# Moving three recurrence units under an earlier projection, with the weights split by column blocks and the rows kept tile by tile

## The reference, cut to what matters

```
h    = layer_norm(x)
q, k, v, x_lru, y_lru = split(h @ w_in)          # widths 512, 128, 128, 512, 512
q, k = rope(rms_norm(q)), rope(rms_norm(k))      # per head of 64
xc   = 4-tap depthwise conv of x_lru along the sequence
r, i = sigmoid(xc @ wa + ba), sigmoid(xc @ wx + bx)       # per head, two directions
a    = exp(-8 r softplus(-lambda));  u = sqrt(1 - a^2) * i * xc
h_fwd, h_bwd = first-order recurrences h = a h + u, forwards and backwards
lru  = (h_fwd + h_bwd) * gelu(y_lru)
```

## Time and profile before

| What | Value |
|---|---|
| profiled execution, its own time | 1866.18 us |
| its span on the core | 1864.5 us |
| granted TensorE clock, mean | 0.91 |
| TensorE busy | 1527.2 us (82%) |
| VectorE busy | 1164.1 us (62%) |
| ScalarE busy | 890.2 us (48%) |
| POOL busy | 512.8 us (28%) |
| stage A, hi part of a tile (L361), 16 times | 1.02 us each |
| stage A, lo part of a tile (L327), 16 times | 1.22 us each |
| stage A, addition on POOL (L294), 16 times, median | 2.39 us each |
| stage A, eviction (L376), 64 times | 0.38 us each |

### The profile page before, as it was taken

The page is one execution under the profiler, slowest core; times in us unless marked ns, Lnnn a source line. Parts: engine busy times, 40 slices in busy tenths (PEclk is TensorE's granted clock), DMA queues, the critical chain, the costliest instruction groups (busy, mean ns, idle before and its releaser), DMA issues. The chain is left out here.

```text
span 1864.5 us, 29928 instructions
## 1 busy us (share of the span) xinstructions
PE 1527.2 (82%) x8888; PEld 1300.7 (70%) x8889; DVE 1164.1 (62%) x2119; ACT 890.2 (48%) x1440; POOL 512.8 (28%) x352
## 2 busy tenths in 40 slices
PE   3999976878854999999999999982599999999700
PEld 3999964656544888888888888861477778778500
DVE  7644339889866866766666677635754444544177
ACT  3323224765674655555555555521255544655222
POOL 2112104342340011121111112111454443545236
PEclk9999988989977999999999999985699999999855
DMA  6655544443414121111112111105378777885562
GB/s 237 225 200 203 195 114 130 142 136 116 144 56 155 45 75 52 51 51 73 52 52 79 51 51 51 63 34 180 113 229 265 218 190 220 236 242 110 101 267 115
DMA packets 143232, 247.96 MB, mean 133 GB/s; under 512 B 18240, under 2 KB 100160, under 8 KB 141120
## 3 DMA queue, kind: packets, MB, share of 16 engines
q1 hardware_dynamic: 115280, 159.59, 25.5%
q0 software_dynamic: 12528, 45.62, 10.4%
q10 hardware_dynamic: 15360, 41.95, 5.8%
HBM read 152.75 MB, written 94.37 MB: 133 GB/s over the span
## 5 line engine op out<-in xcount | busy, mean ns | idle before, releaser
L1312 DVE TENSOR_TENSOR d_probs_t_lo<-d_pt_ps,d_probs_t_hi 128x512 fp32r<-128x512 f32 x256 | 164.2, 683 | 118.7 <-ACT d_probs_t_hi L1254 118.0
L1254 ACT ACTIVATE d_probs_t_hi<-d_pt_ps 128x512 fp32r<-128x512 f32 x256 | 139.3, 596 | 151.6 <-PE d_pt_ps L1141 145.3
L107 PE MATMUL acc<-k_hi,wl_hi 128*128 128x256 f32 x512 | 148.7, 290 | 20.0 <-DVE k_lo L327 9.6
L1298 DVE TENSOR_REDUCE d_neg_max<-d_s_ps 128x1 f32<-128x1024 f32 x128 | 155.3, 1213 | 5.7 <-PE d_s_ps L1130 5.7
L1159 PE MATMUL d_ot_ps<-d_probs_t_hi,d_v_split 128*128 128x256 f32 x512 | 139.2, 306 | 13.1 <-DVE d_probs_t_lo L1312 10.7
L107 PE MATMUL e_a_ps<-up_hi,e_xt_hi 128*128 x336 | 138.9, 413 | 12.9 <-issue 10.6
L108 PE MATMUL acc<-k_lo,wl_hi 128*128 128x256 f32 x512 | 147.3, 288 | 0.0
L109 PE MATMUL acc<-k_hi,wl_lo 128*128 128x256 f32 x512 | 147.2, 288 | 0.0
L1237 ACT ACTIVATE d_probs<-d_s_ps,d_neg_max 128x1024 f32<-128x1024 f32 x128 | 143.2, 1119 | 3.6 <-DVE d_neg_max L1298 3.6
L1141 PE MATMUL d_pt_ps<-ident,d_probs 128*128 128x128 f32 x1024 | 134.2, 274 | 4.4 <-ACT d_probs L1237 3.2
L108 PE MATMUL e_a_ps<-up_lo,e_xt_hi 128*128 x336 | 134.7, 401 | 0.0
(11 more groups left out here) (300 smaller groups left out, 4176.6 us busy)
## 6 DMA issues: line engine op xcount, KB each, us to landing
up_raw<-in_exp_w SPq DMA_DIRECT2D x32, 1024.0 KB, 10.3
down_raw<-in_exp_w SPq DMA_DIRECT2D x16, 1024.0 KB, 11.7
h_dram<-d_h_tile SPq DMA_DIRECT2D x17, 512.0 KB, 2.7
sum_dram<-d_h_tile SPq DMA_DIRECT2D x17, 512.0 KB, 3.5
h_dram<-v_all ACTq DMA_DIRECT2D x16, 512.0 KB, 3.8
ht_hi_dram<-k_hi ACTq DMA_DIRECT2D x8, 1024.0 KB, 5.3
ht_lo_dram<-k_lo ACTq DMA_DIRECT2D x8, 1024.0 KB, 6.6
c_hi<-ht_hi_dram SPq DMA_DIRECT2D x16, 512.0 KB
```

The source lines that it names most:

```text
L107: pe.matmul(out, lhs[0], rhs[0], start=first, stop=False)
L1254: act.activation(pt_hi[:, c * HALF:(c + 1) * HALF, h % 2], pt_ps[c][:], ACT.Copy).then_inc(pth_done[c], 1)
L1298: dve.tensor_reduce(nm[:, u, h:h + 1], s_ps[h % 2][:], AX, ALU.max, negate=True).then_inc(nm_done, 1)
L1312: dve.tensor_tensor(pt_lo[:, part, h % 2], pt_ps[c][:], pt_hi[:, part, h % 2].bitcast(F32), ALU.subtract)\
```

## The change

Stage A becomes `project_xy`. The functions of a unit move into a class `Lru`, which both stages use. The first three units run in stage A beside chunks 4 to 7 (the first sequence is complete after chunk 3), the other five in stage B, one for three tiles (`EVERY = 3`). In stage A:

- The weights are loaded and split in four blocks of 256 columns (all 8 row blocks at once), in place of eight row blocks; products of feature blocks 0 and 1 need only the first.
- Four accumulators become two; the two banks that come free are the gates' `gp`. One `xy` buffer in place of two. The unit's large tiles lie in the raw weights' space.
- The two tiles of a chunk share one chain of small VectorE instructions (`stats` and the rest are twice as wide).
- The transposes of the next chunk follow feature block 3 (block 5 in chunk 0). The loops are written out.
- The small vectors, gate weights and softplus move here, between tile loads 5 and 6 and behind chunks 2 and 3.
- `ht_hi_dram` and `ht_lo_dram` hold one tile per entry, so that stage B reads a tile in whole rows.

In stage B a step is one tile: the rsqrt chain runs for each tile, and the orders of all queues are new. The parts of a unit are spread over three steps.

The core of the diff (the class `Lru` holds the unit's old instructions unchanged; what is only moved is left out):

```
-        acc = [ps(f"acc{j}", [P, 512]) for j in range(4)]
+        acc = [ps(f"acc{j}", [P, 512]) for j in range(2)]
+        gp = [ps(f"gpa{j}", [P, 512]) for j in range(2)]
...
+            transpose(0)                                  # TensorE, stage A
+            for c in range(NC):
+                for f in range(NF):
+                    project(c, f)                         # waits acc_free >= 8c + f - 1
+                    if f == turned_after(c) and c + 1 < NC:
+                        transpose(c + 1)
+                j = c - FIRST                             # FIRST = 4
+                if 0 <= j < len(units):
+                    if j == 0:
+                        pe.wait_ge(gw_in, 128)
+                    lru.gates(pe, j, units[j])
...
+            split(0)                                      # ScalarE, stage A
+            normalise(0)
+            split(1)
+            store_lo = turn(0)
+            split(2)
+            split(3)
+            store_lo()
+            normalise(1)
+            for c in range(NC):
+                j = c - FIRST
+                if 0 <= j - 1 < len(units):
+                    lru.root(act, j - 1)
+                for f in range(NF):
+                    evict(c, f)
+                    if f == turned_after(c):
+                        if c + 1 < NC:
+                            store_lo = turn(c + 1)
+                        if c + 2 < NC:
+                            normalise(c + 2)
...
+                if 0 <= j < len(units):
+                    lru.tanhs(act, j, units[j])
+                    lru.decays(act, j, units[j])
...
+            norms(0); split(0); gain(0); turn(0)          # VectorE, stage A (one per line)
+            split(1); norms(1); split(2); gain(1); split(3)
+            for c in range(NC):
+                j = c - FIRST
+                if j == 0:
+                    lru.conv(dve, link, 0, units[0])
+                if j >= 0 and j + 1 < len(units):
+                    lru.conv(dve, link, j + 1, units[j + 1])
+                if 0 <= j - 1 < len(units):
+                    lru.factor(dve, j - 1)
+                if c + 1 < NC:
+                    turn(c + 1)
+                if 0 <= j - 1 < len(units):
+                    lru.scans(dve, link, j - 1)
+                    lru.output(dve, j - 1)
+                if c + 2 < NC:
+                    norms(c + 2)
+                    gain(c + 2)
...
+                if 0 <= j < len(units):
+                    lru.gated_x(dve, j)
...
-            for g in range(PERIODS):                      # TensorE, stage B
-                front(2 * g)
-                if g:
-                    back(2 * g - 2)
-                front(2 * g + 1)
-                if g:
-                    back(2 * g - 1)
-                gates(g)
+            for t in range(NT):
+                front(t)
+                if t:
+                    back(t - 1)
+                if t % EVERY == 1 and t // EVERY < len(units):
+                    lru.gates(pe, t // EVERY, units[t // EVERY])
...
+            for t in range(NT):                           # ScalarE, stage B
+                if t:
+                    split(t - 1)
+                if t % EVERY == 0 and 0 < t // EVERY <= len(units):
+                    lru.root(act, t // EVERY - 1)
+                square(t)
+                if t:
+                    evict(t - 1)
+                if t % EVERY == 1 and t // EVERY < len(units):
+                    lru.tanhs(act, t // EVERY, units[t // EVERY])
+                    lru.decays(act, t // EVERY, units[t // EVERY])
...
+            for t in range(NT):                           # VectorE, stage B
+                j = t // EVERY
+                if t:
+                    rotate(t - 1)
+                if t % EVERY == 0 and 0 < j <= len(units):
+                    lru.scans(dve, link, j - 1)
+                if t % EVERY == 1:
+                    if 0 < j <= len(units):
+                        lru.output(dve, j - 1)
+                    if j + 1 < len(units):
+                        lru.conv(dve, link, j + 1, units[j + 1])
+                if t % EVERY == 2 and j < len(units):
+                    lru.gated_x(dve, j)
+                    lru.factor(dve, j)
+                norms(t)
```

More of the change, by code:

```diff
@@ L304, in ln, with norms @@
+            def norms(c):
                 for j in range(2):
@@ new lines, in norms, with gain @@
+                link(last)
+                if c:
+                    dve.wait_ge(xn_done, 2 * c)
+                link(dve.tensor_scalar(var[:], mv[:, :, 1], LN_EPS, None, ALU.add))
+                rsqrt(dve, link, var[:], rstd[:], tmp[:])
+                link(dve.tensor_tensor(tmp[:], mv[:, :, 0], rstd[:], ALU.mult))
+                dve.tensor_scalar(shift[:], tmp[:], -1.0, None, ALU.mult).then_inc(stats_done, 1)
+            def gain(c):
+                for j in range(2):
+                    t = 2 * c + j
+                    dve.wait_ge(xn_done, t + 1)
+                    if c:
+                        dve.wait_ge(h_stored[j], 16 * c)
+                        dve.wait_ge(tr_done, t - 1)
+                    else:
+                        dve.wait_ge(ln_sem, 32)
@@ new lines, in _ @@
+            norms(0)
+            split(0)
+            gain(0)
+            turn(0)
+            split(1)
+            norms(1)
+            split(2)
+            gain(1)
+            split(3)
+            for c in range(NC):
+                j = c - FIRST
+                if j == 0:
+                    lru.conv(dve, link, 0, units[0])
[3 more added lines that the diff above has]
+                    lru.factor(dve, j - 1)
+                if c + 1 < NC:
+                    turn(c + 1)
[5 more added lines that the diff above has]
+                    gain(c + 2)
+                if c == 2:
+                    abs_lam()
+                if c == 3:
+                    softplus()
+                if 0 <= j < len(units):
+                    lru.gated_x(dve, j)
@@ L757, in _ @@
-            root(NU - 1)
-            evict(NT - 2)
+            for t in range(NT):
+                if t:
[8 more added lines that the diff above has]
+                    lru.decays(act, t // EVERY, units[t // EVERY])
@@ L759, in _ @@
+            split(NT - 1)
             evict(NT - 1)
@@ L859, in rotate @@
                 dve.tensor_tensor(rt[u], rt[u], rb[u], ALU.add).then_inc(rt_done, 1)
[L861 to L876 removed]
+            lru.conv(dve, link, 0, units[0])
+            for t in range(NT):
+                j = t // EVERY
+                if t:
[11 more added lines that the diff above has]
+                norms(t)
+            rotate(NT - 1)
+            if NT // EVERY == len(units) and NT % EVERY == 1:
+                lru.output(dve, len(units) - 1)
         @block.gpsimd
         def _(pool):
[L880 removed]
             pool.wait_ge(rows_in, 48)
@@ L916, in split @@
                                    k_st[u][:, 0].bitcast(F32), ALU.subtract).then_inc(lo_done, 1)
-            for g in range(PERIODS):
-                for step in (swap, split):
-                    for t in (2 * g, 2 * g + 1):
-                        step(t)
+            for t in range(NT):
+                swap(t)
+                split(t)
 def need(eng, sem, value):
```

735 lines of the change are left out of this document (350 added, 385 removed).

## The result

The changed kernel takes 1943.04 us (median of four runs, 1940.96 to 1948.18), the kernel before 1864.0 beside it: a ratio of 1.0432, 95% interval 1.04 to 1.0464. The forecast was 1941. The profiled execution took 1943.3 us, with a span of 1941.6 and a mean granted clock of 0.893 (0.91 before).

The account below looks back on a forecast made before the run. TensorE bounds the first projection and VectorE the second stage, with a ring through ScalarE close behind. Stage A +93.7 and stage B -16.4, together +77.3, on the median 1863.38 gave 1941 us; 8-in-10 range 1893 to 1970.

Parts of the forecast that it names:

- Start: Start of stage A: TensorE's first product at 25.4 us instead of 32.68, 7.3 us sooner, a lead that doesn't last.
- second gain: VectorE's second gain instruction before the first product: 3.46 us, because POOL's addition stands beside it.
- Ordinary chunks: Stage A, chunks 1 to 4: block 6 waits 6.8 us for evict 4, clock loses 1.7, making 33.3 us a chunk.
- slow starts: TensorE after each stall in stage A: lower granted clock loses 1.7 us a stall.
- rival (4): TensorE's clock stays low after each stall through two blocks, 4.1 us more at ten stalls: 1982 us, chance 0.08.
- rival (3): First chunks of stage A don't stall, two accumulators being enough, 5 x 8.5 us less: 1898 us, chance 0.08.
- Chunks with units: Stage A, chunks 5 to 7: copies wait behind unit work and norms; 60.6, 41.3 and 39.5 us, last product at 340.6.
- Table loads: ScalarE's table loads: 1.28 us each; the skill page's extra drain, an estimated 23 us in all, left out.
- Stage B: Second stage: 52.7 us per three tiles, 302.1 us in all, a change of -16 us.
- my two terms: Stage B on VectorE: eight more chains, 22 us, and a 4.2 us root wait in each period.
- Rival (1): Both stages: units fill idle time and nothing waits, stage A +1, stage B -59 us: 1805 us, chance 0.09.
- Rival (2): Stage B's ring is looser than worked out and waits vanish, 43 us less: 1898 us, chance 0.10.

Follow-up runs that it names:

- norms ahead: Changed kernel with norms and normalise of chunk c + 2 ahead of the transposes of chunk c + 1 on VectorE and ScalarE: 1891.9 us.
- four banks: Changed kernel with four accumulators instead of two for chunks 0 to 3, queue order unchanged: 1918.4 us.
- root first: Changed kernel with the root in stage B ahead of the split on ScalarE: 1931.7 us.
- pairs in B: Changed kernel with stage B back in periods of two tiles, its five units in the first five periods: 1917.2 us.
- best A with pairs in B: Changed kernel with norms ahead, stage A's decays and root later on ScalarE, and stage B in periods of two tiles: 1850.1 us.

## Why the prediction was right, step by step

- **Start.** First product 25.4 forecast, 24.31 measured. The second gain took 1.22 us (at 14.18), not 3.46: POOL's first addition, which I had put ahead of it, began 0.24 us behind it (at 14.42), and it was POOL's that stretched. Chunk 1 started at 60.94 (64.3), block 2 at 34.86 (36.8). A small miss, never made up: the products of chunk 4 ended at 196.1 (199.2), 3.1 us early.
- **Ordinary chunks.** From the start of chunk 1 to the end of chunk 4 it took 135.2 us (134.9 forecast), 33.8 a chunk. The gaps were 6.01, 5.26, 6.69 and 7.21, mean 6.3 (6.8 forecast; its terms add up to 14.2 and not 14.3, so 6.7). The stretch holds five slow starts, one behind the gap ahead of chunk 1, as in the forecast, and 10.8 us are left for them (135.2 less four times 24.8 and the 25.2 of gaps): 2.2 each where I had 1.7. The two errors cancel. In the windows view chunk 1 (64 to 99) has 0.87 of the clock, where the same stretch before had 1.00: after a stall matmuls go at the lower rate again. The clock does recover within the chunk (0.50 from 61 to 64, 1.00 from 67 to 70; 0.53 from 88.6 to 94, 1.00 from 94 to 100), so rival (4), with 5.8 us a stall, falls. That the stall comes from norms standing ahead of the copy is shown by norms ahead, and that two banks are too few to cover it is shown by four banks; rival (3) falls with the gaps above.

```profile
64.00:99.00 35.00, 28.98 (x216) 28.78 (x215) 9.93 (x25) 7.26 (x12) 7.96 (x4) 0.87 0.64 240
```

- **Chunks with units.** Chunk 5 lasted 61.3 us (196.09 to 257.37, the starts of its gates; 60.6 forecast), with gaps of 7.47 and 15.91 (7.2 and 17.3). ScalarE's timeline has the first as I built it, decays, table, root, and only then the copy:

```profile
204.93 2.37 ACT L272 ACTIVATE wl_raw<-wl_raw,half_decay 128x1024 f32<-128x1024 f32 x2
207.31 1.28 ACT L276 ACT_TABLE_LOAD   x1
208.61 2.37 ACT L276 ACTIVATE wl_raw<-wl_raw,nhalf_decay 128x1024 f32<-128x1024 f32 x2
...
215.28 1.91 ACT L282 ACTIVATE wl_raw<-wl_raw 128x2048 f32<-128x2048 f32 x1 [1.06 <-DVE wl_raw L306]
217.10 0.64 ACT L556 ACTIVATE xy<-acc 128x256 f32<-128x256 f32 x2
```

  Chunk 6 lasted 43.2 (41.3 forecast) and chunk 7 ended with the stage's last copy at 341.24 (last product 340.6 forecast). The three chunks took 0.7, 1.9 and 1.2 us more than forecast, which makes up for the early start. Stage A: +94.3 measured, +94 forecast.
- **Table loads.** 1.28 us, with the next instruction 1.30 behind the start of the load (207.31, 208.61 above). The drain that the Trainium skill, "ScalarE: Activation LUTs", section What ACT_TABLE_LOAD costs, adds isn't seen here either: the load of 207.31 starts 0.02 us behind the end of the instruction ahead of it. So leaving out the 23 us was right.
- **Stage B.** Period 52.93 (52.7), root wait 4.23 (4.2), swap 1.25 (1.2), length 301.5 (302.1): -17.0, forecast -16. (The 34.9 us of a period before are the mean between the first and the last unit's products; between factors it is 35.4, which changes nothing in the sum.) Root first and pairs in B show the mechanism: a chain per tile and the waits in the order take back most of what three units less would give. I had priced these at 22 us of chains and 21 of root waits. Taking both away with the pairs brought 26.6, so my two terms are not additive; the removed time partly shows up as other waits, those for the squares.
- **Rival (1)**, units that fill idle time, falls twice. As built, the copies stand behind the unit; and in the best order found, three units moved still lose 12.5 us of the median. The rule cited with it (Trainium skill, "Perfetto Trace Analysis", section Optimization Strategy, that stages with different contended engines may gain from interleaving) brought nothing here in any order tried: TensorE, which the first projection is short of, also has the unit's gates to do, and the copies that it waits for share ScalarE's queue with the unit. **Rival (2)** falls with the period.

The mechanism was the forecast one. That the sums came out within 1 us is partly luck: chunks 0 to 4 came 3.1 us early and chunks 5 to 7 took 3.8 too long, the gaps were shorter and the slow starts longer than I had them, and in stage B a tail 2 us shorter made up for periods and a start that were a little longer.

## What to carry to other kernels

Before work is put beside a stage, follow for each engine's queue what stands ahead of the one instruction that the bounding engine waits for (here a 0.38 us copy out of an accumulator), and compare that chain with the work that the buffers cover. Try a copy that frees a buffer ahead of everything that has its own wait; reordering alone was worth 67 us of stage A here (54.6 and 12.6). And price the moved work in both places: the best version keeps the early start, the vectors prepared ahead and the order, and moves no unit at all. That holds for the orders tried here; one without the gaps behind the gates was not.

## What the hardware showed that I had not expected

Scans of VectorE and subtractions of POOL slow each other: beside POOL's split a scan of 1024 columns took 3.27 and 2.75 us, alone 2.29 and 2.27, and POOL's two instructions 2.30 and 2.71 us instead of 1.28 and 0.73. The times look as if they took turns: the four would take 6.57 us one after the other, and in the run root first the last of them ends at 465.10, 5.97 us behind VectorE's product (459.13); POOL's second one, which starts at 460.24 beside the running scan, ends 0.52 us behind that scan's end. POOL's first one already begins beside the product, and its delay is not the scan's. I had let that happen to plain two-input operations only. The other finding is the clock after a gap. The windows view of the run best A with pairs in B, ahead of its gap of 4.84 us and twice behind it (columns as above), has the granted clock at 1.00, 0.50 and 1.00, which is 2.4, 1.2 and 2.4 GHz; the first of these stretches stands behind a gap of 1.13 us:

```profile
183.00:188.00 5.00, 5.00 (x44) 5.00 (x44) 2.95 (x3) 4.02 (x5) 0.00 (x0) 1.00 0.41 145
193.50:199.00 5.50, 5.50 (x26) 5.50 (x27) 5.43 (x4) 0.20 (x2) 0.00 (x0) 0.50 0.01 4
199.50:202.00 2.50, 2.50 (x23) 2.50 (x22) 2.47 (x3) 0.00 (x0) 0.00 (x0) 1.00 0.04 16
```

The slow stretch holds 26 matmuls in 5.5 us where the first holds 44 in 5.0: 2.5 us lost (5.5 less 26 x 0.114). In the changed kernel the stalls of 5.3 to 15.9 us in stage A cost 1.6 to 2.8 us each beside the gap, a longer gap not always more; a gap of 2.39 in the run best A with pairs in B cost 1.6, and one of 1.13 only 0.1.
